# A product with one column of ones in place of a product with 32 and a transpose, for the softmax denominators

## What is computed

```python
def block_attention(q, k, v, scale):
        s = jnp.einsum('bqkgd,blkd->bkgql', qblk, k).astype(jnp.float32) * scale
        p = jax.nn.softmax(s, axis=-1).astype(v.dtype)
        return jnp.einsum('bkgql,blkd->bqkgd', p, v)
...
    o_a = block_attention(ql_a, jnp.concatenate([kc_a, kl_a], 1), jnp.concatenate([vc_a, vl_a], 1), GQA_SCALE)
    ...
    if not ctx_out:
        return xl_new, None
    oc_a = block_attention(gqa_q(gq_c, p["gqa_q_g"], None), kc_a, vc_a, GQA_SCALE)
```

## Time and profile before

| | before |
|---|---|
| median of 3 runs | 947.19 us |
| lowest, highest | 946.35, 947.42 us |
| the profiled execution's own time | 949.86 us |
| its span, first to last instruction | 948.0 us |
| mean granted TensorE clock | 0.992 of full speed |

### The profile page before, as it was taken

How to read it: one execution, slowest core, us unless ns; L and a number is a source line. 1 busy time by engine, 2 the same in 40 slices (tenths; PEclk the granted TensorE clock), 3 DMA queues, 4 the chain that set the end, 5 groups by cost and what they waited for, 6 DMA issues and landing times.

```text
span 948.0 us, 13381 instructions
## 1 busy us (share of the span) xinstructions
PE 908.3 (96%) x4629; PEld 641.7 (68%) x4629; DVE 557.3 (59%) x903; ACT 429.8 (45%) x879; POOL 511.1 (54%) x433
## 2 busy tenths in 40 slices
PE   5999999999999999999999899999999999999996
PEld 3778667889744565665678779888884445555684
DVE  5569033523678679963318838567246758983337
ACT  5332121414556466655334853235335645655432
POOL 3247223324577755565547438455538886566672
PEclk9999999999999999999999999999999999999998
DMA  9957662213623200010353212222343221020242
GB/s 318 291 214 261 211 249 75 73 45 100 142 53 92 60 18 18 18 68 1 129 189 112 98 31 82 86 65 84 79 120 78 69 50 26 18 76 1 104 164 88
DMA packets 51913, 96.13 MB, mean 101 GB/s; under 512 B 9540, under 2 KB 24752, under 8 KB 50824
## 3 DMA queue, kind: packets, MB, share of 16 engines
q1 hardware_dynamic: 51848, 95.29, 32.7%
HBM read 71.61 MB, written 4.21 MB: 80 GB/s over the span
## 4 chain that ended last, share of the span: by engine, by line
PE 79%; DVE 8%; ACT 6%; issue 2%; POOL 2%; DMA 1%; SPq 1%; POOLq 0%; ACTq 0%; DVEq 0%
PE banks L1003 14%; PE banks L1005 13%; PE banks L1004 13%; PE banks L1300 12%; PE banks L1322 11%; PE banks L1245 4%; ACT area_z L1859 2%; PE banks L1014 2%; PE banks L1341 2%; DVE negmax L2254 2%; PE banks L1274 1%; PE banks L1334 1%; DMA w_raw<-in_w_in_dram 1%; ACT late_bias L1836 1%; DVE area_b L2431 1%
## 5 line engine op out<-in xcount | busy, mean ns | idle before, releaser
L1968 POOL TENSOR_TENSOR w_split<-w_raw,w_split 128x512 fp32r<-128x512 f32 (+4 forms) x122 | 148.7, 1226 | 217.1 <-ACT w_split L1577 215.4
L1003 PE MATMUL banks<-w_split,area_a 128*128 128x512 f32 (+3 forms) x612 | 232.1, 379 | 5.7 <-issue 2.7
L1005 PE MATMUL banks<-w_split,area_a 128*128 128x512 f32 (+3 forms) x612 | 224.7, 367 | 0.0
L1004 PE MATMUL banks<-w_split,area_a 128*128 128x512 f32 (+3 forms) x612 | 224.0, 366 | 0.0
L2254 DVE TENSOR_REDUCE negmax<-banks 128x1 f32<-128x768 f32 x160 | 148.2, 951 | 79.1 <-PE banks L1245 55.8
L1577 ACT ACTIVATE w_split<-w_raw 128x512 fp32r<-128x512 f32 (+4 forms) x122 | 69.1, 582 | 195.4 <-PE banks L1005 185.9
L1695 ACT ACTIVATE area_z<-banks 128x512 f32<-128x512 f32 x196 | 108.3, 599 | 75.9 <-PE banks L1300 72.7
L1003 PEld LDWEIGHTS banks<-w_split,area_a 128*128 128x128 f32 x612 | 115.3, 188 | 38.8 <-issue 21.2
L1300 PE MATMUL banks<-area_a 97*128 97x512 f32 (+4 forms) x448 | 128.4, 401 | 4.2 <-ACT area_z L1695 3.1
L1005 PEld LDWEIGHTS banks<-w_split,area_a 128*128 128x128 f32 x612 | 115.2, 188 | 16.5
L1004 PEld LDWEIGHTS banks<-w_split,area_a 128*128 128x128 f32 x612 | 115.6, 189 | 12.8
(11 more groups left out here) (238 smaller groups left out, 1443.2 us busy)
## 6 DMA issues: line engine op xcount, KB each, us to landing
w_raw<-in_w_in_dram SPq DMA_DIRECT2D x32, 512.0 KB, 3.6
area_g<-in_w_ada_dram SPq DMA_DIRECT2D x13, 1024.0 KB, 6.3
area_g<-in_w_ada_dram SPq DMA_DIRECT2D x16, 512.0 KB, 5.9
w_raw<-in_w_out_dram SPq DMA_DIRECT2D x16, 512.0 KB, 4.3
area_a<-parts SPq DMA_DIRECT2D x72, 96.0 KB, 2.2
area_a<-parts SPq DMA_DIRECT2D x30, 192.0 KB, 3.6
area_b<-in_x_dram SPq DMA_DIRECT2D x8, 512.0 KB, 7.6
w_raw<-in_w_in_dram SPq DMA_DIRECT2D x8, 352.0 KB, 5.5
```

The lines of the kernel that those rows point to most:

```text
L1003: nc.tensor.matmul(dst, a[0], b[0], start=first, stop=False)
L1004: nc.tensor.matmul(dst, a[0], b[1], start=False, stop=False)
L1005: return nc.tensor.matmul(dst, a[1], b[0], start=False, stop=last)
L1968: op = nc.gpsimd.tensor_tensor(lo, raw, hi.bitcast(F32), ALU.subtract)
```

## The change

The stationary and the moving operand change places. For each tile of 128 queries, the sums (`total`) are the stationary operand, 128 x 128, and one column of ones is streamed; the result is one column of 128 partitions, which already has the queries on the partitions. In layer 0 the context's queries have two tiles of keys each, added in the bank by two products. The ring entry "dt", the copy on ACT, the four transposes, the buffers `d_s` and `scr`'s second half for this use, and the semaphore d_copied go. DVE takes one reciprocal of 12 (layer 0) or 8 (layer 1) columns straight from the bank of "d". The ring entry "d" is free when rec_done says so.

```diff
-            RING += [("dt", _L, _p - 1)] + [("o", _L, _p - 1, g) for g in ((1, 0) if ctx else (1,))]
+            RING += [("o", _L, _p - 1, g) for g in ((1, 0) if ctx else (1,))]
...
                     elif k[0] == "d":
-                        pe.wait_ge(d_copied, PN[k[1:]] + 1)
-                    elif k[0] == "dt":
                         pe.wait_ge(rec_done, PN[k[1:]] + 1)
...
             def denominators(L, p):
+
                 pe.wait_ge(dve_summed, N_DVE_SUM[L, p, 1])
                 dst = ring_slot("d", L, p)
-                for u in range(2):
-                    mm = nc.tensor.matmul(dst[32 * u:32 * u + 32, :], ones_c[:], total(L, p, u), start=True, stop=True)
-                if L < DEPTH - 1:
+                one = ones_c[:, 0:1]
+                for n, t in enumerate(q_tiles(L)):
                     for u in range(2):
-                        mm = nc.tensor.matmul(dst[64 + 32 * u:96 + 32 * u, :], ones_c[:], prob(L, p, "ctx", u), start=True, stop=True)
-                mm.then_inc(ring_filled, 1)
-
-            def turn_denominators(L, p):
...
+                        out_col = dst[:, 2 * n + u:2 * n + u + 1]
+                        if t < CT:
+                            for kt in range(CT):
+                                nc.tensor.matmul(out_col, prob(L, p, "ctx", u)[:, kt * NCTX + t * P:kt * NCTX + (t + 1) * P], one,
+                                                 start=(kt == 0), stop=(kt == CT - 1))
+                        else:
+                            mm = nc.tensor.matmul(out_col, total(L, p, u)[:, (t - CT) * P:(t - CT + 1) * P], one,
+                                                  start=True, stop=True)
                 mm.then_inc(ring_filled, 1)
...
                     scores(L, p, 3)
                     max_tile(L, p + 2, 0)
-                    turn_denominators(L, p - 1)
                     turn_output(L, p - 1)
...
                     exponent(L, p, 2)
-                    copy_denominators(L, p - 1)
                     exponent(L, p, 3)
...
-                r = N_RINGB["dt", L, p] - 1
+                r = N_RINGB["d", L, p] - 1
                 dve.wait_ge(ring_filled, r + 1)
-                turned = banks[:, r % NRING, :].rearrange("p (i u n) -> p i u n", i=TILES - CT, u=4)
...
-                    chain(nc.vector.tensor_reduce(d_s[:], both, AX.X, ALU.add))
-                    nc.vector.reciprocal(rec[:, 0:2 * CT].rearrange("p (t u) -> p t u", u=2), d_s[:])
-                nc.vector.reciprocal(rec[:, k - 2 * (TILES - CT):k].rearrange("p (t u) -> p t u", u=2),
-                                     turned[:, :, 0:2, 0]).then_inc(rec_done, 1)
+                nc.vector.reciprocal(rec[:, 0:2 * len(ts)], banks[:, r % NRING, 0:2 * len(ts)]).then_inc(rec_done, 1)
```

More of the change, by code:

```diff
@@ L478, in hybrid_layers @@
         ones_c = sb("ones_c", [P, 32])
-        d_s = sb("d_s", [P, 2, 2])
         row_sum = sb("row_sum", [P, TILES, 4])
@@ L506, in hybrid_layers @@
         z_rows = area_b[:, 4 * NTOK:4 * NTOK + TILES * 352].rearrange("p (t n) -> p t n", t=TILES)
-        d_rows = scr[:, 1, :]
         raw_tiles = w_raw[:].rearrange("p s k n -> p (s k) n")
@@ L575, in hybrid_layers @@
         rec_done = sem("rec_done")
-        d_copied = sem("d_copied")
         combined = sem("combined")
@@ L1494, in last_pair @@
                 out_step(L, 1, latents)
-                turn_denominators(L, p)
                 turn_output(L, p)
@@ L1712, in copy_context @@
                 copy(o_t[:, 0:NCTX], banks[:, r % NRING, 0:NCTX]).then_inc(ctx_copied, 1)
[L1714 to L1720, removed]
             def squares(L, p):
@@ L1827, in attend @@
                     copy_context(L, NPAIR - 1)
-                copy_denominators(L, NPAIR - 1)
             def square_rows(kind, L, t):
@@ L2294, in output_rows @@
                 ts = q_tiles(L)
-                r = N_RINGB["dt", L, p] - 1
+                r = N_RINGB["d", L, p] - 1
                 dve.wait_ge(ring_filled, r + 1)
-                turned = banks[:, r % NRING, :].rearrange("p (i u n) -> p i u n", i=TILES - CT, u=4)
-                k = 2 * len(ts)
-                if L < DEPTH - 1:
-                    both = banks[:, r % NRING, :].rearrange("p (h t x n) -> p t x n h", h=2, t=CT, x=4)[:, :, 2:4, 0, :]
-                    chain(nc.vector.tensor_reduce(d_s[:], both, AX.X, ALU.add))
-                    nc.vector.reciprocal(rec[:, 0:2 * CT].rearrange("p (t u) -> p t u", u=2), d_s[:])
-                nc.vector.reciprocal(rec[:, k - 2 * (TILES - CT):k].rearrange("p (t u) -> p t u", u=2),
-                                     turned[:, :, 0:2, 0]).then_inc(rec_done, 1)
+                nc.vector.reciprocal(rec[:, 0:2 * len(ts)], banks[:, r % NRING, 0:2 * len(ts)]).then_inc(rec_done, 1)
                 dve.wait_ge(rec_done, n + 1)
```

## The result

The changed kernel takes 1001.78 us, the median of 4 runs (1001.62 to 1005.11), beside 946.95 us for the kernel before in the same comparison: a ratio of 1.0576, 95% interval 1.0559 to 1.0593. That is +54.8 us where the forecast said +22.8. The sign was right and the size was not; the time lies above the stated range of 954 to 994.

The account below looks back on a forecast made before the run. PE, busy 96% of the span, was taken to bound the kernel. Load pace +25.2, hidden -1.6 and -2.0, moved wait +1.2 gave +22.8 us, so 970 us, range 954 to 994.

Parts of the forecast that it names:

- Pace of the loads: PE's denominator series: 0.111 us per weight load, 3.55 us a pair in layer 0, 1.78 in layer 1.
- rival 2: Denominator loads follow at 0.064 us, like those of transposes: 950 us; chance 0.08, shared with paces up to 0.1.
- rival 4: Each denominator load waits for the stream ahead, 0.15 to 0.19 us: 990 to 1008; chance 0.08, with paces 0.13 to 0.15.
- rival 5: Each one-column denominator product is issued once, not twice: 240 loads, 26.6 us, no change, 947; chance 0.03.
- Sum without the clock: Whole kernel, no fall of the clock: +25.2 - 1.6 - 2.0 + 1.2 = +22.8 us; chance 0.55.
- +4.0 - 1.6 = +2.4: Layer 1: ten pairs' loads less the work that goes, +4.0 us, less 1.6 hidden in two waiting pairs.
- 21.2 - 2.0 + 1.2 = +20.4: Layer 0: loads less work that goes +21.2 us, 2.0 hidden in two pairs, 1.2 for waits on the reciprocal.
- -2.0 for the two waiting pairs: Layer 0, pairs at 350.82 and 375.13: about 1 us of 2.12 vanishes in each, 0 to 4 us together.
- The hidden part: Waits of PE cover some new work: -1.6 us in two layer 1 pairs, -2.0 in two layer 0 pairs.
- The moved wait: Output transposes wait for DVE's reciprocal behind the context maximum in three layer 0 pairs: 0.5 + 0.5 + 0.2 = +1.2 us.
- the first rival: Clock falls to 1.2 GHz after layer 0's series: 15 us, 985; with half of layer 1's, 993; chance 0.23.
- The main forecast of 970: Whole kernel with no fall of the clock: 970 us, own range 963 to 978; chance 0.55.

Follow-up runs that it names:

- experiment 1: The changed kernel with each product streaming 128 equal columns of ones in place of one, in both layers: 966.15 us, ratio 1.0199 to the kernel before.
- experiment 6: The kernel before with the change in layer 1 alone, streaming 128 columns of ones in place of one: 946.63 us, ratio 0.9986 to the kernel before.

## Why the prediction was wrong

**Pace of the loads: right.** 3.55 us for 32 records was forecast and found where the clock stays up; in layer 1 it is 1.70 for 16, where 1.78 was forecast. Rivals 2, 4 and 5 fall: no pace of 0.064, none of 0.15, and 32 records and not 16.

**Sum without the clock: nearly right.** Experiments 1 and 6 split it by layer. Layer 1 costs -1.3 us (forecast +4.0 - 1.6 = +2.4), so layer 0 costs 18.6 + 1.3 = about +20 (forecast 21.2 - 2.0 + 1.2 = +20.4). Layer 0 is right in sum; its -2.0 for the two waiting pairs was a guess, and no run tests it apart. Layer 1 is 3.7 us too high. Three terms can be read: the pace (0.08 x 8 pairs = 0.6); what the old products and the old small transposes cost ahead of their own start, 0.1 us each (some 2 us in ten pairs); and the fall at 799 in the kernel before (1.7 us). Against them stand the 0.6 us of the next paragraph. The second is read from starts in layer 1, the kernel before first, experiment 6 second:

```profile
740.99 1.22 PE L1300 MATMUL banks<-area_a 128*128 128x512 f32 x4
...
743.12 1.20 PE L1300 MATMUL banks<-area_a 128*128 128x512 f32 x4
744.24 0.46 PE L1352 MATMUL banks<-ident,scr 64*128 64x64 f32 x4
```

```profile
739.62 1.20 PE L1307 MATMUL banks<-area_a 128*128 128x512 f32 x4
740.66 1.95 PE L1357 MATMUL banks<-ones_c,w_raw 128*128 128x128 f32 x16
742.37 1.19 PE L1307 MATMUL banks<-area_a 128*128 128x512 f32 x4
743.40 0.60 PE L1341 MATMUL banks<-ident,o_t 128*128 128x128 f32 x4
```

From the scores to the denominators are 1.14 us before (740.99 to 742.13) and 1.04 in experiment 6; from the next scores to what follows them are 1.12 us where small transposes follow and 1.03 where they don't. I took what the old work holds from its own start on, which leaves this out. No run tests it alone.

**The hidden part: right in kind.** The two waiting pairs of layer 1 do swallow the series. In experiment 6 they start 1.97 us apart, not 1.89, and PE waits for the reciprocal behind them, 0.6 us in all, which the forecast had only in layer 0.

**The moved wait: right in sum, by luck in part.** PE's wait for rec is 1.4 us in 4 places in experiment 1 (+1.2 forecast), but 0.8 of it stand in two pairs of layer 0, where three were forecast, and 0.6 in layer 1, where none was. In the changed kernel itself it is 0.3 us: PE arrives later there.

**The step that failed is the clock: the sum put it at nothing, and the first rival had its chance and its price too small.** The prediction held that "loads may count as work: no row says so", gave the fall 0.23, and priced it at 15 us for layer 0 and 23 with half of layer 1. Experiment 1 shows 35.6 us. By layer, the experiments give about 23 us for layer 0 (42.8 with its change alone, less the 20 that it costs without the falls) and 11 for layer 1 (10.2 + 1.3), where the prediction had 15 and 8. Each size in that estimate was too small. A fall was taken to last the 3 us of the earlier trace rows, 1.5 us lost; six of layer 0's ten last 6.8 us or more (292.1 to 299 above), and one minus the granted clock over its ten adds up to 29 us. In layer 1 eight of ten series have a fall, where half were allowed, though the series is half as long; they add up to 15 us (the kernel before has two falls there, 3.4 us). Why 29 and 15 us come to no more than 35.6 us of time, no run shows. The main forecast of 970 is, within 4 us, the time with 128 columns, where attention has no falls: 966.15.

What could have been read beforehand: the earlier trace rows show a fall behind a stretch where PE was partly idle, and so does the window at 799, which I had not read; the pair at 817 shows that such a stretch need not bring one. The section "What's actually happening" of the page "TensorE: Matmul & The Clock Gate" in the Trainium skill says that activity of the engine releases the clock. I had weighed that rule as open as to loads. The runs settle it for this kernel: PE's timeline is just as full with one column as with 128, the loads are the same, and with one the clock falls to 0.50 while with 128 it stays at 1.00 in both attention stretches.
